# Half of the context squares on ScalarE, modulation blocks loaded one phase earlier, PSUM scratch for more inverse roots, one product of the difference attention on GpSimd, and high-part products first where three half-blocks begin together

## The reference, cut to what matters

```
first_block:   x += s5_mixer(rmsnorm(x))                 # state space mixer, then y @ w_glu, gated
               x += relu(rmsnorm(x) @ mlp_w1)**2 @ mlp_w2
               x += (p @ ple_w) * sigmoid(rmsnorm(x) @ ple_gate_w)
               x  = rmsnorm(x) * norm_final
second_block:  mod = silu(c) @ w_ada + b_ada             # for x, and again for the context, two layers
  per layer:   hx, hc = rms_norm(x)*gain*(1+scale)+shift, the same for ctx
               four branches from hx @ w_in: Fourier, convolution with layer norm and silu,
                 grouped attention, difference attention (p0 - lam*p1) @ v, then rms_norm per head
               x += g * (sum(gates * branches) @ w_out)
               x += g * swiglu(rms_norm(x)*gain*(1+scale)+shift)   # FFN width 2816
               in layer 0 the context goes through the same, in layer 1 only its keys and values
out = rms_norm(x) * final_norm
```

## Time and profile before

| what | value |
|---|---|
| time, median of 3 runs | 2138.36 us (2131.72 to 2143.5) |
| the profiled execution's own time | 2134.92 us |
| its span | 2133.1 us |
| PE busy | 1965.8 us (92%) |
| POOL, DVE, ACT busy | 1077.8, 1003.0, 747.8 us |
| mean granted TensorE clock | 0.956 of full |
| moved by DMA | 274.01 MB, mean 128 GB/s |

### The profile page before, as it was taken

One profiled execution on the slowest core, in us unless ns is written; L12 is line 12 of the kernel. 1 busy time (PEld: TensorE's weight loads), 2 busy tenths in 40 slices (PEclk: granted clock), 3 DMA queues, 4 the chain that ended last, 5 costly groups with the idle time before them and its releaser, 6 DMA issues.

```text
span 2133.1 us, 32899 instructions
## 1 busy us (share of the span) xinstructions
PE 1965.8 (92%) x13805; PEld 1732.1 (81%) x13805; DVE 1003.0 (47%) x1706; ACT 747.8 (35%) x1212; POOL 1077.8 (51%) x565
## 2 busy tenths in 40 slices
PE   3988899987999999989998999999899998879997
PEld 3756899986798778968776888888798997879997
DVE  7853454125483577484246111112547767473114
ACT  2214354323322552272232222222245525334442
POOL 7004588746344544304433444444367742776885
PEclk9779999988999999999998999999999999989998
DMA  6355577777412213102332223322345331554652
GB/s 148 100 153 178 203 248 254 253 271 232 160 60 84 66 31 121 58 31 89 115 103 79 93 71 96 117 84 75 99 149 159 110 100 39 173 165 143 181 168 82
DMA packets 285734, 274.01 MB, mean 128 GB/s; under 512 B 6458, under 2 KB 283460, under 8 KB 285332
## 3 DMA queue, kind: packets, MB, share of 16 engines
q1 hardware_dynamic: 282164, 265.94, 39.1%
q10 hardware_dynamic: 2688, 4.86, 0.8%
q0 software_dynamic: 736, 1.12, 0.4%
HBM read 265.86 MB, written 4.19 MB: 127 GB/s over the span
## 4 chain that ended last, share of the span: by engine, by line
PE 82%; DVE 9%; ACT 2%; DMA 2%; issue 2%; POOL 1%; SPq 0%; DVEq 0%; ACTq 0%; POOLq 0%
PE gb L2332 18%; PE gb L2333 17%; PE gb L2334 17%; PE gb L1351 4%; PE gb L1353 3%; PE gb L1352 3%; PE gb L1559 3%; PE gb L1560 3%; PE gb L1558 3%; PE mb L2469 1%; PE mb L612 1%; PE mb L1099 1%; DVE mx L1128 1%; DMA raw<-in_w_ada 1%; PE mb L1154 1%
## 5 line engine op out<-in xcount | busy, mean ns | idle before, releaser
L2320 POOL TENSOR_TENSOR wl<-raw,wh 128x1024 fp32r<-128x1024 f32 (+3 forms) x452 | 982.4, 2192 | 927.2 <-ACT wh L731 926.4
L731 ACT CAST wh<-raw 128x1024 fp32r<-128x1024 f32 (+3 forms) x452 | 418.6, 937 | 756.6 <-PE gb L2334 384.8
L2332 PE MATMUL gb<-xh,wh 128*128 128x256 f32 (+1 forms) x1856 | 609.0, 328 | 20.1 <-DVE xl L1045 10.4
L2333 PE MATMUL gb<-xl,wh 128*128 128x256 f32 (+1 forms) x1856 | 605.5, 326 | 0.0
L2334 PE MATMUL gb<-xh,wl 128*128 128x256 f32 (+1 forms) x1856 | 604.9, 326 | 0.0
L2332 PEld LDWEIGHTS gb<-xh,wh 128*128 128x128 f32 x1856 | 358.1, 193 | 55.1 <-issue 19.0
L2333 PEld LDWEIGHTS gb<-xl,wh 128*128 128x128 f32 x1856 | 358.2, 193 | 27.6
L2334 PEld LDWEIGHTS gb<-xh,wl 128*128 128x128 f32 x1856 | 357.9, 193 | 27.9
L1351 PE MATMUL gb<-wh,xh 128*128 128x256 f32 x608 | 174.4, 287 | 1.4 <-POOL wl L2320 1.4
L1353 PE MATMUL gb<-wl,xh 128*128 128x256 f32 x608 | 172.8, 284 | 0.0
L1352 PE MATMUL gb<-wh,xl 128*128 128x256 f32 x608 | 172.7, 284 | 0.0
(11 more groups left out here) (447 smaller groups left out, 3050.6 us busy)
## 6 DMA issues: line engine op xcount, KB each, us to landing
raw<-in_w_in SPq DMA_DIRECT2D x62, 1024.0 KB, 5.3
raw<-in_w_ada SPq DMA_DIRECT2D x48, 1024.0 KB, 6.8
raw<-in_w_ffn SPq DMA_DIRECT2D x44, 1024.0 KB, 5.1
raw<-in_mlp_w SPq DMA_DIRECT2D x32, 1024.0 KB, 6.2
raw<-in_w_ffn SPq DMA_DIRECT2D x16, 768.0 KB, 4.6
raw<-in_w_ffn SPq DMA_DIRECT2D x16, 640.0 KB, 4.2
raw<-in_ssm_w_glu SPq DMA_DIRECT2D x8, 1024.0 KB, 6.9
raw<-in_w_out SPq DMA_DIRECT2D x8, 1024.0 KB, 5.1
```

The source lines that it names most:

```text
L731: nc.scalar.copy(split_half(wh, p, j, h), raw_half(p, it, j, h)).then_inc(hi_ready, 1)
L2320: nc.gpsimd.tensor_tensor(split_half(wl, p, j, h), raw_half(p, it, j, h), split_half(wh, p, j, h).bitcast(F32), ALU.subtract)\
L2332: nc.tensor.matmul(o, H[:, k, :], XH, start=st, stop=False)
L2333: nc.tensor.matmul(o, H[:, k, :], XL, start=False, stop=False)
```

## The change

Six edits, some at several places:

- **Context squares.** POOL squares the first four tiles of the context, ACT the last four (two `Square` instructions into `sqr` and `cxsq2` in the last step of `ple`). PE sums six tiles instead of two in norm 2 (12 matmuls of one column instead of 4). In `ple`, `split_first=False` puts ACT's casts for layer 0 behind the last block's steps and the square of the norm.
- **Modulation blocks.** The 4 blocks between `ple`'s weights move to `mlp2` (behind its blocks 2, 6, 10 and 14).
- **Inverse roots.** Norms 3, 4, 6 and 7 and `merge_heads` take `rsqrt_beside`; in `merge_heads` and norm 2 the result is left in PSUM.
- **Diagonals of norm 2.** Six `tensor_scalar` of 128 columns become three `tensor_tensor` of 256.
- **Difference attention.** The product with p1 goes to POOL (`diff_pool`: a one-column product with lambda, then the row), and DVE issues the reciprocal of an item ahead of the next item's maxima and the last product behind them.
- **Order in `leading`.** For each tile the two products with the operand's high part are issued for all half-blocks after a wait for `xh` alone, then, after the wait for `xl`, the product with the low part.

```diff
-        INLINE = [(name, i) for name, n in (("mlp1", 16), ("mlp2", 16), ("ple", 8)) for i in range(1, n, 2)]
+        INLINE = [(name, i) for name, n in (("mlp1", 16), ("mlp2", 16)) for i in range(1, n, 2)]
+        INLINE += [("mlp2", i) for i in (2, 6, 10, 14)]
...
             pe.wait_ge(s_cq, 1)
+            pe.wait_ge(s_ca, 2)
             for t in range(2):
                 for i in range(2):
-                    ins = nc.tensor.matmul(mb[:, t, 2:3], cxsq[:, 2 + i, t * P:t * P + P], ones[:, 0:1],
-                                           start=(i == 0), stop=(i == 1))
+                    nc.tensor.matmul(mb[:, t, 2:3], cxsq[:, 2 + i, t * P:t * P + P], ones[:, 0:1],
+                                     start=(i == 0), stop=False)
+                for i in range(4):
+                    sq = (sqr[:, i, SEQ:SEQ + CTX] if i < 2 else cxsq2[:, i - 2, :])[:, t * P:t * P + P]
+                    ins = nc.tensor.matmul(mb[:, t, 2:3], sq, ones[:, 0:1], start=False, stop=(i == 3))
...
-            if n in (0, 1, 5, 8):
...
+            ps = gb[:, 1, 448:464] if n in (0, 1, 5, 8) else mb[:, nt - 1, 448:464]
+            rsqrt_beside(T1, rs[:, 0, 0:nt], rs[:, 1, 0:nt], ps[:, 0:nt], ps[:, 8:8 + nt], wide=dg[:, 0:nt, :])
...
-            rsqrt_beside(T1, six[0], six[1], *(gb[:, 1, 448 + 8 * i:454 + 8 * i] for i in range(2)))
+            inverse = gb[:, 1, 464:470]
+            rsqrt_beside(T1, six[0], six[1], *(gb[:, 1, 448 + 8 * i:454 + 8 * i] for i in range(2)), last=inverse)
+            y = inverse.rearrange("p (t c) -> p t c", c=3)
+            wide = ident.unsqueeze(1).to_broadcast([P, 2, P])
             for c in (1, 2):
-                for t in range(2):
-                    T1.add(v.tensor_scalar(dg2[:, 2 * (c - 1) + t, :], ident, y[:, t, c:c + 1], None, ALU.mult))
+                T1.add(v.tensor_tensor(dg2[:, 2 * (c - 1):2 * c, :], wide, y[:, :, c:c + 1].to_broadcast([P, 2, P]),
+                                       ALU.mult))
...
+        def diff_pool(pool, l, P1):
+            for n in items(l, "d"):
+                c = ITEMS[n][5]
+                pool.wait_ge(s_r2, diff_index(n) + 1)
+                p1 = probs[:, (c + 1) % PROBS, 0:nk(n)]
+                P1.add(nc.gpsimd.tensor_tensor(mx[:, 2, (c + 1) % 8:(c + 1) % 8 + 1],
+                                               mx[:, 2, (c + 1) % 8:(c + 1) % 8 + 1], lamb[:, l:l + 1], ALU.mult))
+                P1.wait()
+                nc.gpsimd.tensor_tensor(p1, p1, mx[:, 2, (c + 1) % 8:(c + 1) % 8 + 1].to_broadcast([P, nk(n)]),
+                                        ALU.mult).then_inc(s_p1, 1)
...
             for i in range(len(mine) + 1):
+                if i >= 1:
+                    difference(mine[i - 1])
                 if i < len(mine):
                     for c in scores_of(mine[i]):
                         row_maximum(dve, mine[i], c)
                 if i < 2:
                     transposes_dve(dve, l, "d", 4 + 2 * i, 6 + 2 * i)
                 if i >= 1:
-                    difference(mine[i - 1])
+                    weighted(mine[i - 1])
...
-                rsqrt(D1, st[:, 1, 0:n], st[:, 2, 0:n], st[:, 3, 0:n], st[:, 0, 0:n], st[:, 0, 0:n], 1.0 / P, EPS)
+                step(v.tensor_scalar(st[:, 1, 0:n], st[:, 0, 0:n], 1.0 / P, EPS, ALU.mult, ALU.add))
+                inverse = mb[:, 3, 384:512][:, 64:64 + n]
+                rsqrt_beside(D1, st[:, 1, 0:n], st[:, 2, 0:n], mb[:, 3, 384:512][:, 0:n], mb[:, 3, 384:512][:, 32:32 + n], last=inverse)
...
+                if 4 * it + j == 7:
+                    act.wait_ge(s_cxc, 2)
+                    for i, dst in enumerate((sqr[:, 0:2, SEQ:SEQ + CTX], cxsq2[:, :, :])):
+                        nc.scalar.activation(dst, x[:, 4 + 2 * i:6 + 2 * i, SEQ:SEQ + CTX], ACT.Square)\
+                            .then_inc(s_ca, 1)
             gemm_act(act, p_pl, pair_tanh(act, p_pl, SEQ), context_copy,
-                     lambda: squares_act(act, 2, sqr))
+                     lambda: squares_act(act, 2, sqr), split_first=False)
...
-                    for f in range(0, KD, 2):
+                    for f in range(0, KD // 2, 2):
...
                 for k in range(kt):
-                    need(0, 0, k)
+                    high(k)
                     XH, XL = X(0, k)
                     for j, b in lead:
-                        ins = products(gview(p, j, T)[:, b, :], split_half(wh, p, j, b), split_half(wl, p, j, b), k,
-                                       XH, XL, k == 0 and (b == 0 or T > 256),
-                                       k == kt - 1 and ((j, 1 - b) not in lead or b == 1 or T > 256))
+                        o = gview(p, j, T)[:, b, :]
+                        nc.tensor.matmul(o, split_half(wh, p, j, b)[:, k, :], XH,
+                                         start=k == 0 and (b == 0 or T > 256), stop=False)
+                        nc.tensor.matmul(o, split_half(wl, p, j, b)[:, k, :], XH, start=False, stop=False)
+                    need(0, 0, k)
+                    for j, b in lead:
+                        ins = nc.tensor.matmul(gview(p, j, T)[:, b, :], split_half(wh, p, j, b)[:, k, :], XL,
+                                               start=False, stop=k == kt - 1 and
+                                               ((j, 1 - b) not in lead or b == 1 or T > 256))
```

More of the change, by code:

```diff
@@ L424, in build @@
         s_cq = sem("context_squares_ready")
+        s_ca = sem("context_squared_by_scalar")
         s_pl = sem("p_lo")
@@ L901, in rsqrt, with rsqrt_beside @@
                 step(v.scalar_tensor_tensor(y, t, 1.5, y, ALU.add, ALU.mult))
-        def rsqrt_beside(T1, ms, y, yp, t, wide=None):
+        def rsqrt_beside(T1, ms, y, yp, t, wide=None, last=None):
             def step(ins):
@@ L918, in rsqrt_beside @@
                     return
-                step(v.scalar_tensor_tensor(yp if i < 2 else y, t, 1.5, y, ALU.add, ALU.mult))
+                step(v.scalar_tensor_tensor(yp if i < 2 else y if last is None else last, t, 1.5, y,
+                                            ALU.add, ALU.mult))
         def rms_dve(dve, T1, n, dg, count, eps):
@@ L931, in rms_head_dve @@
             total = mb[:, 0:nt, 0:1].rearrange("p a b -> p (a b)")
-            if n in (0, 1, 5, 8):
[L933 to L939, removed]
+            T1.add(nc.vector.tensor_scalar(rs[:, 0, 0:nt], total, 1.0 / count, eps, ALU.mult, ALU.add))
+            T1.wait()
+            ps = gb[:, 1, 448:464] if n in (0, 1, 5, 8) else mb[:, nt - 1, 448:464]
+            rsqrt_beside(T1, rs[:, 0, 0:nt], rs[:, 1, 0:nt], ps[:, 0:nt], ps[:, 8:8 + nt], wide=dg[:, 0:nt, :])
             T1.wait()
@@ L954, in first_rms_dve @@
             T1.wait()
[L955 removed]
+            inverse = gb[:, 1, 464:470]
+            rsqrt_beside(T1, six[0], six[1], *(gb[:, 1, 448 + 8 * i:454 + 8 * i] for i in range(2)), last=inverse)
+            y = inverse.rearrange("p (t c) -> p t c", c=3)
+            wide = ident.unsqueeze(1).to_broadcast([P, 2, P])
             for c in (1, 2):
[L957 to L958 removed]
+                T1.add(v.tensor_tensor(dg2[:, 2 * (c - 1):2 * c, :], wide, y[:, :, c:c + 1].to_broadcast([P, 2, P]),
+                                       ALU.mult))
             T1.wait()
             dve.sem_inc(s_dg, 1)
[L961 to L962 removed]
+            T1.add(v.tensor_tensor(dg1[:, 0:2, :], wide, y[:, :, 0:1].to_broadcast([P, 2, P]), ALU.mult))
             T1.wait()
@@ L1285, in difference, with weighted @@
                 dve.wait_ge(s_ex, c + 2)
-                D1.add(v.reciprocal(mx[:, 2, c % 8:c % 8 + 2], mx[:, 1, c % 8:c % 8 + 2]))
-                D1.wait()
+                if diff_index(n) >= 4:
+                    dve.wait_ge(s_p1, diff_index(n) - 3)
+                v.reciprocal(mx[:, 2, c % 8:c % 8 + 2], mx[:, 1, c % 8:c % 8 + 2]).then_inc(s_r2, 1)
+            def weighted(n):
+                c = ITEMS[n][5]
                 p0, p1 = probs[:, c % PROBS, 0:nk(n)], probs[:, (c + 1) % PROBS, 0:nk(n)]
-                D1.add(v.tensor_scalar(p1, p1, mx[:, 2, (c + 1) % 8:(c + 1) % 8 + 1], lamb[:, l:l + 1],
-                                       ALU.mult, ALU.mult))
-                D1.wait()
+                dve.wait_ge(s_p1, diff_index(n) + 1)
                 v.scalar_tensor_tensor(p0, p0, mx[:, 2, c % 8:c % 8 + 1], p1, ALU.mult, ALU.add).then_inc(s_wd, 1)
             for i in range(len(mine) + 1):
+                if i >= 1:
+                    difference(mine[i - 1])
                 if i < len(mine):
@@ L1385, in layer_pe @@
                 norm_pe(pe, n0, sqr2, dg2)
-            gemm_pe(pe, q["cv"], T, X2(T), first_use(pe, s_xl, op0[n0]), lead=THREE)
+            gemm_pe(pe, q["cv"], T, X2(T), first_use(pe, s_xl, op0[n0]), lead=THREE,
+                    high=lambda k: pe.wait_ge(s_xh, op0[n0] + k + 1))
             heads_pe(pe, l, "zf", nt)
@@ L1451, in layer_pe @@
                     gemm_pe(pe, q["f1", half, i], T, X2(T), None if half else first_use(pe, s_xl, op0[n0 + 2]),
```

(8 more changed lines are left out.)

15 lines of the change are left out of this document (10 added, 5 removed).

## The result

| | before | after |
|---|---|---|
| median of 6 runs | 2135.49 us (2131.72 to 2143.5) | 2120.44 us (2117.58 to 2124.97) |
| ratio, 95% interval | | 0.9929 (0.9909 to 0.9948) |
| profiled execution, own time and span | 2134.92, 2133.1 | 2124.96, 2123.2 |
| PE busy | 1965.8 us | 1979.0 us (93%) |
| POOL, DVE, ACT busy | 1077.8, 1003.0, 747.8 us | 1104.0, 961.5, 749.9 us |

15 us faster (0.7%, with an interval clear of 1), 3.4 us above the forecast and inside its range. How the -15 comes about is another matter: of the six terms those of parts 1, 2 and 5 were wrong, and the clock, which the sum held still but at one place, moved at several.

What follows compares the result with a forecast made beforehand. The prediction took PE, busy 92% of the span, as the bound. Terms -5.2 (parts 1 to 3), -10.1, -4.3 and -0.6 gave -20.2 us, so 2114.7 or 2118.2; it took 2117, range 2107 to 2128 for 8 in 10.

Steps and rivals of the forecast that it cites:

- Part 1: Modulation blocks moved: +4.7 us in `mlp2`, against -3.5 behind block 1 and -1.2 at the end of `ple`.
- Part 2: Context squares: -4.6 us for the context's copy, -0.55 for POOL's squares, +3.7 for 16 more sums.
- the plus sign: From `mlp2` to `cv`, the gains of Part 1 and Part 2 were added in full, within -5.2 us for parts 1 to 3.
- Part 3: Diagonals of norm 2: two `tensor_tensor` at 0.85 us instead of four `tensor_scalar` at 4.44, worth -3.7.
- The bound for "waits for POOL": At norm 2, the new diagonals would gain 0 instead of -3.7 us if they wait for POOL as before.
- Part 4: Inverse roots: norm 4 -2.4 us, norm 7 -3.3, `merge_heads` of layer 1 -4.4; together -10.1.
- Part 5: High parts first: PE starts 0.5 to 1.0 us sooner at phase starts and keeps the gain; together -4.3.
- rival (b): Starts: starting earlier only meets another wait, hiding Part 5 and half of parts 1 to 3; +7 us, 2124; chance 0.09.
- Part 6: Difference attention: pitch of maxima 2.46 us with 512 keys, 1.75 with 256; together -0.6.
- rival (c): Difference attention: POOL's one-column product is dear; +13 us, 2130; chance 0.08.
- Rival (a): `mlp2`: the ring of loads falls behind, some 4 waits of 1 us with the clock down; +8 to 10, 2126; chance 0.12.
- (d): `mlp2`: DMA can't exceed 253 GB/s, +12 us, and waits lower the clock, +19; 2148, slower than before; chance 0.03.

Runs made afterwards that it cites:

- e8: The changed kernel without the moved modulation blocks and without the split of the context squares; 2121.95 us, ratio 0.9926 to the kernel before.
- e6: The changed kernel with all context squares on POOL and ACT's casts ahead of the context's copy again; 2117.38 us, ratio 0.9914 to the kernel before.
- e3: The changed kernel with its 4 modulation blocks back in `ple` instead of `mlp2`; 2113.27 us, ratio 0.9887 to the kernel before.
- e0: The changed kernel run once more, unaltered, as yardstick; 2120.57 us, ratio 0.9937 to the kernel before.
- e5: The kernel before with only the new inverse roots (norms 3, 4, 6, 7 and `merge_heads`); 2125.20 us, ratio 0.9948 to the kernel before.
- e9: The changed kernel with one small step ahead of norm 2's inverse root taking an operand from PSUM; 2115.80 us, ratio 0.9901 to the kernel before.
- e2: The kernel before with only the new order of products, high parts first; 2137.83 us, ratio 1.0000 to the kernel before.
- e10: The changed kernel with modulation blocks back in `ple`, norm 2's step from PSUM and extra products in PE's waits; 2104.77 us, ratio 0.9850 to the kernel before.
- e11: e10 with the old order of products (three matmuls of each half-block together); 2103.90 us, ratio 0.9829 to the kernel before.
- e1: The changed kernel with the old order of products (three matmuls of each half-block together); 2123.25 us, ratio 0.9936 to the kernel before.
- e4: The changed kernel with the difference attention as before, p1's product on DVE; 2122.72 us, ratio 0.9942 to the kernel before.

## Why the prediction was right, and where it was not

- **Part 1, predicted 0.** Alone it is 0 by L (e8 to e6; the medians say -4.6), beside part 2 it costs 7 by both. The 4.7 in `mlp2` is right, and the modulation block of norm 1 waits 1.1 longer. The "-3.5 and -1.2" in `ple` exist only without part 2: from `ple` to norm 2's first sums e8 takes 46.5, e3 and e6 both 40.0, the changed kernel 38.8: PE finds the new wait of 1.34 behind block 1 and one of 1.10 for the context's first half, which e3 doesn't have. The last 1.3 is lost again before the diagonals.
- **Part 2, predicted -1.45.** Without part 1 it is worth -3.4 of L (e8 to e3) and -8.7 of the median, with it +4 and +3 (e6 to e0; 1.4 of the 4 at norm 3, by chance). The step that failed is the plus sign: parts 1 and 2 remove the same stall, the late load of layer 0's first block, and it can be counted once only. That the stretch from `mlp2` to `cv` still came out at -7.2 against -6.7 predicted is luck: up to norm 2's sums the kernel before takes 2.7 more than e8. The clock in the first 8 us of `ple` is 0.64 against 1.00; but e5, with 0.63, takes only 1.0 more than e8, so 1.8 of the 2.7 is what two executions of the same instructions differ by.
- **Part 3, predicted -3.7.** The term is right (4.44 became 0.75). But the step of two numbers ahead had been free of POOL by luck: 0.17 from 528.23, where POOL's first subtraction gives way to its second (528.30). Now it falls inside one and gives back 2.1. The bound for "waits for POOL" was put on the wrong instruction.
- **Part 4, -10.1.** Right by the median, -9.5 alone; -6.2 by L, without norm 4's 2.4. In `merge_heads` the first step takes 1.14 and the two products 1.29 (1.4 was predicted), and the wait of 2.83 is gone:

```profile
1809.28 1.14 DVE L2027 TENSOR_SCALAR st<-st 128x8 f32<-128x8 f32 x1
1813.34 1.29 DVE L2032 TENSOR_TENSOR dq<-dq,mb 128x512 f32<-128x512 f32 x2
```

- **Part 5, predicted -4.3, is 0 to -2.** The starts come 0.5 to 0.9 sooner as worked out. Behind `mlp1` and `cv` of layer 1 POOL's next half takes it back, as rival (b) has it, to which I had given 0.09; behind `cv` and FFN 0 of layer 0 it is the half clock, which no rival had there.
- **Part 6, -0.6.** Pitch 2.42 and 1.60 against 2.46 and 1.75 predicted; POOL's one-column product takes 0.19, so rival (c) is out. Of the 2.7 that it gains in layer 0, 2.3 are lost in the two stages behind, where the clock is at half for longer. That loss was not in the sum, and the medians can't tell part 6 from 0.
- **Not in the sum:** the clock behind `cv` (+2.4, of which e5 shows 1.6 without any change ahead of `cv`) and behind `wo` up to norm 4's sums (+2.7). The one profile of the kernel before has it full at both.

Rival (a) has one of its waits, in norm 1; (d) is out: DMA moves 280 GB/s from 359 to 477 us with PE at clock 0.99. The forecast came within 3.4 us because half of it, part 4, was read from a twin of the same form, and because the slow `ple` of the kernel before made up for the overlap of parts 1 and 2. Against the medians -20.2 was 5 us too much, which is of the size of part 5 and the clock behind `cv`; against L, which fell by 11.5, it was 9 too much. Single executions don't split this further.

## What to carry to other kernels

Before adding two gains in one stretch, ask what each would be with the other already in place; if both let the same late transfer go, build only the cheaper and test the four combinations. Where PE waits for three microseconds at several places, cheap products in the wait are worth more than starting a microsecond sooner at half clock. A tiny vector step with all operands in SBUF can cost a whole GpSimd instruction; whether it does is settled by where it falls, so its time in one trace is no promise for the next.

## What the runs showed of the hardware

The clock can fall while PE's records show it busy all the time: in norm 2 of the changed kernel, 24 sums of one column run from 521.1 to 525.9. Three microseconds ahead of the fall and three behind it:

```profile
518.00:521.00 3.00, 3.00 (x40) 2.44 (x28) 0.25 (x1) 2.36 (x3) 1.51 (x1) 1.00 0.80 232
522.00:525.00 3.00, 3.00 (x16) 3.00 (x15) 0.00 (x0) 1.99 (x2) 3.00 (x2) 0.50 1.11 392
```

And it can rise while PE does nothing, in the kernel before ahead of `cv`:

```profile
538.00:539.00 1.00, 0.76 (x4) 0.47 (x3) 1.00 (x3) 0.14 (x1) 0.00 (x0) 0.53 1.05 372
539.00:540.00 1.00, 0.00 (x0) 0.00 (x0) 0.81 (x3) 1.00 (x3) 0.00 (x0) 1.00 0.87 306
```

The same instructions can meet it or not. Norm 3 has 32 sums of one column, and PE has no wait in the 35 us ahead of them. The changed kernel's sums and the clock behind them, then e9's sums, behind which it stays at 1.00:

```profile
880.23 4.14 PE L881 MATMUL mb<-ones,sqr 128*128 128x1 f32 x32
```

```profile
884.37:887.37 3.00, 3.00 (x15) 3.00 (x16) 2.38 (x15) 0.00 (x0) 1.93 (x1) 0.50 0.00 1
```

```profile
873.36 3.63 PE L881 MATMUL mb<-ones,sqr 128*128 128x1 f32 x32
```

Some starts follow the kernel in all 14 profiles. At `ple`, in its first 8 us, the clock is 0.63 and 0.64 in the two with the modulation blocks in `ple` and nothing else changed there (before, e5), 1.00 in the five with the blocks there and part 5 or extra products (e2, e3, e8, e10, e11), and 0.76 to 0.80 in the seven with the blocks moved. At `wo` of layer 0 it is 0.51 to 0.54 with part 6. At `cv` it is 0.57 to 0.64 in five with part 2 (after, e0, e1, e3, e4), 0.68 in e9, 0.74 in e6, 1.00 in e2, e8 and the three with extra products, and 1.00 and 0.72 for the same instructions (before, e5). So an edit can move the clock at places that it does not touch, as part 6 does at `wo`; how much of the move at `cv` is the kernel's and how much is chance stays open.
